# A two-block transformer on one Trainium2 core: the second block's first mixer as one stage, and the overflow quads of the experts before the last regular quad

## The chip, the core and the metric

The kernel runs on one core of a Trainium2 chip. The core has TensorE (matrix products into PSUM), VectorE and ScalarE (elementwise work on PSUM and SBUF), GpSimd, and SyncE, whose queue here issues the weight loads. The engines run their own instruction streams and meet only at semaphores. The metric is the device time of one launch in microseconds (us). All data are float32.

## What is computed

A first pair of layers (attention, then pooling, each followed by a mixture of 32 experts with top-2 routing) is followed by a second pair (mixer A+B with a dense feed-forward, then mixer C with another). 256 tokens, 1024 channels. The parts that matter here, cut:

```python
def expert_block(args):                      # per layer, tokens sorted by expert
    xb, e = args
    return (jax.nn.silu(xb @ w1[e]) * (xb @ w3[e])) @ w2[e]

def s5_ssm(u, ...):                          # 32 groups of 16 channels, 64 complex states each
    bu_re = jnp.einsum('blgp,gnp->blgn', ug, bb_re)
    bu_im = jnp.einsum('blgp,gnp->blgn', ug, bb_im)
    _, _, x_re, x_im = lax.associative_scan(_complex_affine_combine, (a_seq_re, a_seq_im, bu_re, bu_im), axis=1)
    y = jnp.einsum('blgn,gpn->blgp', x_re, c_re) - jnp.einsum('blgn,gpn->blgp', x_im, c_im)
    return y + d_skip * ug

def mixer_ab(x, ...):
    proj = x @ w_in                          # three blocks of 512: xm, zm, us
    xc = jax.nn.silu(causal_dwconv(xm, conv_w, conv_b))
    q, k, v = block-diagonal maps (4x4 blocks) of xc, xc, xm
    gates = jnp.concatenate([q, k, v], axis=-1) @ w_if + b_if
    h = mlstm_chunkwise(q, k, v, gates[..., :4], gates[..., 4:])       # 4 heads of 128
    hn = layer norm of h over each head, * mh_gain
    out_m = (hn + skip * xc) * jax.nn.silu(zm)
    y = jax.nn.gelu(s5_ssm(us, ...))
    out_s = y * jax.nn.sigmoid(y @ w_glu + b_glu)
    return jnp.concatenate([out_m, out_s], axis=-1) @ w_out
```

## The kernel before

The program is a list of stages. In each a function per engine gives its instructions; at its end every engine drains and adds one to `stage_done`, and all wait for all four before the next stage (`run_stages`, L236). Weights stream from HBM through a ring of six slots of 2 MB (`ring_buffer`); SyncE issues every load when `weights_used`, which TensorE increments, shows that the slot's last unit was consumed.

**Experts** (`experts(layer, lead)`, twice). Each expert has a block of 32 token slots; four blocks make a quad, so one quad fills the 128 partitions. A quad needs 12 units of 2 MB (24 MB), twice the ring. Eight regular quads (`FIRST_QUADS`) hold all 32 experts; quad 1 is the wide quad, whose four experts each get a second block (`_b`) on the same weights. For experts with still more tokens there are four overflow quads (`MORE // QUAD`). Whether one is live is only known at run time (`quad_live`, written by `table_dve`). Every engine runs `each_quad`: a loop over quads 2 to 7, then a loop over the four overflow quads that reads `quad_live`; for a dead one it only drains and increments each semaphore of the quad once. SyncE does the same in `load_experts`, where a dead quad waits until TensorE has consumed all 96 units. TensorE's quad is: turn the weights of the picks (L1283), `up` of w1 (two phases) and w3 (two phases, L1272), gather the next quad's tokens (L1245), turn the product (L1288), `down` (two phases, L1297), `combine` (L1311) into PSUM banks 0 to 3. In the wide quad `up` and `down` run for both blocks before a unit's slot is released.

**Mixer A+B** (`mixer_ab`) is seven stages: projections (L1877; VectorE copies the tiles, then convolves, L1901 and L1904), q/k/v and gates (L1932 to L1941; VectorE takes the 12 tiles, L1949), gate sums and the running maximum (L1970 to L2008), four heads (L2030 to L2080), layer norm (L2098 to L2124), the state space in four quarters (L2147 to L2200), and the GLU (L2214 to L2226). In a quarter TensorE makes real and imaginary inputs of four groups of pairs (`states`), VectorE turns them by the angle of each time step (L2173 to L2179), runs eight scans (L2182, L2183), turns back (L2185 to L2188) and adds (L2189, L2190), and TensorE multiplies by C (`outputs`, L2156, L2157); VectorE adds the skip (L2194) and ScalarE applies GELU (L2200). `project_out` (L1754) follows.

`chain["dve"]` (`v(...)` below) makes an instruction increment a semaphore and the engine wait for it before the next.

## Time and profile before

| | us |
|---|---|
| median of 3 runs | 2293.22 (2293.07 to 2293.73) |
| the profiled execution's own time | 2287.05 |
| span of the profiled execution | 2285.2 |
| busy share of the span: TensorE, VectorE, ScalarE, GpSimd | 76%, 23%, 9%, 4% |
| of it, the seven stages of mixer A+B (1348.34 to 1549.80) | 201.5 |

The profile is of one execution. Times in it count from the start of the span. TensorE's `PEclk` is the granted clock: 1.00 is 2.4 GHz, 0.50 is 1.2 GHz.

### The profile page before, as it was taken

The page shows a single profiled execution, that of the slowest core. Times are in us where ns is not written, and L with a number is a line of the kernel's source. Part 1 is how long each engine was busy: PE and PEld are TensorE (multiplying, and loading weights), DVE is VectorE, ACT ScalarE, POOL GpSimd, SP SyncE. Part 2 cuts the span into 40 slices and gives each one's busy share as a digit, 9 for nine tenths or more (in the row PEclk, how much of TensorE's full clock was granted, in tenths as well). Part 3 has the DMA queues.
Part 4 walks back from the last instruction along what each step waited for, and adds up shares of the span by engine and source line. Part 5 has one row for each costly group of instructions (what it writes and reads, how often), then busy time and mean ns, then how long its engine had stood idle before and what let it go on. Part 6 is the DMA issues. An engine that isn't in the chain of part 4 may idle for free. (4 is left out here: it accounts for less than half of the span.)

```text
span 2285.2 us, 22430 instructions
## 1 busy us (share of the span) xinstructions
PE 1728.7 (76%) x8954; PEld 997.7 (44%) x8955; DVE 522.8 (23%) x1188; ACT 208.2 (9%) x489; POOL 93.5 (4%) x120
## 2 busy tenths in 40 slices
PE   6999867766666566876666658218999989889998
PEld 3655533321222343322222247114886476648863
DVE  1214352110111164111011132882000023320001
ACT  1011110000000110000000011002000122110000
POOL 1010010000000037000000000000000000000000
PEclk9999989887878778887787878558999999789999
DMA  9969179999999748999999951006335334124330
GB/s 367 378 247 388 74 297 389 397 422 422 422 422 422 295 174 336 381 420 422 422 422 422 386 172 42 1 10 220 119 117 188 142 137 146 63 83 147 111 129 19
DMA packets 125764, 581.02 MB, mean 254 GB/s; under 512 B 14004, under 2 KB 18392, under 8 KB 70264
## 3 DMA queue, kind: packets, MB, share of 16 engines
q1 hardware_dynamic: 120416, 573.90, 62.8%
q10 hardware_dynamic: 4344, 3.25, 0.5%
q0 software_dynamic: 928, 2.79, 0.4%
q8 instruction: 56, 0.92, 0.2%
q14 instruction: 20, 0.16, 0.0%
HBM read 578.86 MB, written 1.05 MB: 254 GB/s over the span
## 5 line engine op out<-in xcount | busy, mean ns | idle before, releaser
L1272 PE MATMUL ps<-ring_buffer,arena 128*32 128x512 f32 x2048 | 312.5, 767 | 198.9 <-DMA ring_buffer<-in_exp_w 196.1
L1796 PE MATMUL ps<-hT,ring_buffer 128*128 128x256 f32 x1408 | 310.9, 383 | 4.1 <-issue 2.6
L1796 PEld LDWEIGHTS ps<-hT,ring_buffer 128*128 128x128 f32 x1408 | 269.4, 192 | 45.5 <-issue 6.3
L1272 PEld LDWEIGHTS ps<-ring_buffer,arena 128*32 128x32 f32 x2048 | 85.0, 136 | 412.6 <-issue 336.2
L1297 PE MATMUL ps<-ring_buffer,arena 128*32 128x512 f32 x1088 | 155.9, 726 | 101.2 <-DMA ring_buffer<-in_exp_w 90.1
L1804 PE MATMUL ps<-ring_buffer,arena 128*128 128x512 f32 x352 | 154.2, 595 | 3.0 <-DVE arena L1837 1.9
L1297 PEld LDWEIGHTS ps<-ring_buffer,arena 128*32 128x32 f32 x1088 | 41.0, 130 | 204.9 <-issue 196.7
L1466 DVE TENSOR_TENSOR arena<-arena,ps 128x512 f32<-128x512 f32 x18 | 19.2, 1069 | 439.9 <-PE ps L1272 439.9
L1804 PEld LDWEIGHTS ps<-ring_buffer,arena 128*128 128x128 f32 x352 | 65.9, 190 | 90.4 <-issue 87.8
L1245 PE MATMUL ps<-arena,xn 128*128 128x128 f32 x640 | 81.9, 289 | 12.4 <-DVE arena L1436 12.4
L1245 PEld LDWEIGHTS ps<-arena,xn 128*128 128x128 f32 x640 | 78.5, 203 | 27.9 <-issue 22.2
L2276 PE MATMUL ps<-hT,ring_buffer 128*128 128x256 f32 x384 | 85.9, 385 | 1.9 <-issue 1.0
L1837 DVE TENSOR_TENSOR arena<-arena,ps 128x256 f32<-128x256 f32 x44 | 18.5, 421 | 296.9 <-ACT arena L1831 296.9
L2276 PEld LDWEIGHTS ps<-hT,ring_buffer 128*128 128x128 f32 x384 | 73.6, 193 | 14.7 <-issue 3.5
L1387 ACT ACTIVATE arena<-ps,mod,gain 128x128 f32<-128x128 f32 x72 | 27.1, 457 | 436.5 <-PE ps L1245 436.5
L713 PE MATMUL ps<-hT,ring_buffer 128*128 128x256 f32 x256 | 58.6, 391 | 3.1 <-ACTq L236 2.5
L1754 PE MATMUL ps<-ring_buffer,hT 128*128 128x512 f32 x128 | 58.1, 613 | 2.1 <-DVEq L236 1.9
L1311 PE MATMUL ps<-arena 128*128 128x512 f32 x128 | 59.3, 605 | 0.0
L1482 DVE TENSOR_TENSOR arena<-ps,gates 128x512 f32<-128x512 f32 x16 | 11.1, 692 | 198.9 <-PE ps L1297 198.9
L498 PE MATMUL ps<-ring_buffer,arena 128*32 128x512 f32 x384 | 49.6, 637 | 8.0 <-DMA ring_buffer<-in_ada_w 7.1
L713 PEld LDWEIGHTS ps<-hT,ring_buffer 128*128 128x128 f32 x256 | 50.0, 197 | 13.0 <-issue 3.3
L2156 PE MATMUL ps<-ring_buffer,arena 128*32 128x256 f32 x32 | 4.4, 634 | 57.3 <-DVE ring_buffer L2190 57.3
(493 smaller groups left out, 1566.9 us busy)
## 6 DMA issues: line engine op xcount, KB each, us to landing
ring_buffer<-in_exp_w SPq DMA_DIRECT2D x384, 1024.0 KB, 18.5
ring_buffer<-in_ffn_w SPq DMA_DIRECT2D x30, 2048.0 KB, 9.0
ring_buffer<-in_ada_w SPq DMA_DIRECT2D x24, 2048.0 KB, 12.8
ring_buffer<-in_c_w_in SPq DMA_DIRECT2D x8, 2048.0 KB, 9.1
ring_buffer<-in_attn_w_in SPq DMA_DIRECT2D x6, 2048.0 KB, 16.8
ring_buffer<-in_ab_w_in SPq DMA_DIRECT2D x3, 2048.0 KB, 12.8
ring_buffer<-in_ffn_w SPq DMA_DIRECT2D x6, 1024.0 KB, 9.2
ring_buffer<-in_attn_w_o SPq DMA_DIRECT2D x2, 2048.0 KB, 12.9
```

The lines of the kernel that those rows point to most:

```text
L498: pe.matmul(ps[g * WIDE:(g + 1) * WIDE, COND, :], spread_c[:, 2 * pair + k, row:row + WIDE], w[:, k, 512 * n:512 * (n + 1)], start=(first ...
L713: ins = pe.matmul(ps[:, n % BANKS, 0:S], w[:, k, j * P:(j + 1) * P], hT[:, k, :], start=(k == 0), stop=(k == KD - 1))
L1245: ins = pe.matmul(ps[:, BXA + k // 4, (k % 4) * P:(k % 4 + 1) * P], xn[:, t, k * P:(k + 1) * P], pick[:, t, :], start=(t == 0), stop=(t == ...
L1272: ins = pe.matmul(ps[c, bank, :], tokens[:, 4 * phase + k, c], halves[j][:, k, :], start=(phase == 0 and k == 0), stop=(phase == 1 and k = ...
L1297: ins = pe.matmul(ps[c, bank, :], tokens[:, 2 * phase + k, c], halves[j][:, k, half * 512:(half + 1) * 512], start=(phase == 0 and k == 0) ...
L1311: ins = pe.matmul(ps[:, 2 * half + t, :], weights[:, t, :], values[:, half * 512:(half + 1) * 512], start=opens, stop=False, skip_group_ch ...
L1387: return eng.activation(o, src, ACT.Identity, scale=G[:, k:k + 1], bias=H[:, k:k + 1])
L1466: dve.tensor_tensor(prod.rearrange("c (h k p) -> c h p k", h=2, k=2), gated.rearrange("c (h p k) -> c h p k", h=2, k=2), ps[:, bank, :].re ...
L1754: ins = pe.matmul(ps[:, 2 * c + t, :], fT[:, k, t * P:(t + 1) * P], w[:, k, :], start=(k == 0), stop=(k == KD - 1))
L1796: ins = pe.matmul(ps[:, f % 8, i * S:(i + 1) * S], w[:, k, j * P:(j + 1) * P], hT[:, k, :], start=(k == 0), stop=(k == KD - 1))
L1804: ins = pe.matmul(ps[:, 2 * half + t, :], aT[:, r + k, t * P:(t + 1) * P], w[:, k, 512 * half:512 * half + 512], start=(r + k == 0), stop= ...
L2276: ins = pe.matmul(ps[:, n % 8, 0:S], w[:, k, j * P:(j + 1) * P], hT[:, k, :], start=(k == 0), stop=(k == KD - 1))
```

## The change

1. **Mixer A+B is one stage.** The projection order is us, xm, zm. ScalarE now copies every projection, q/k/v and gate tile out of PSUM (`take_tile`), through three rotating banks (4 to 6). VectorE runs the four state-space quarters with the steps of the other branch in between; TensorE's instructions are interleaved by hand. GELU is one instruction over all four quarters, and the GLU's sigmoid follows the layer norm's square root.
2. **Last sums by TensorE.** VectorE no longer makes the two sums at the end of a quarter (L2189, L2190 before). It writes four products, and TensorE accumulates four products with C in place of two.
3. **Dead quads moved.** The overflow quads come before quad 7, on every engine and on SyncE, with semaphores of their own for their weights (`more_landed`, `more_used`); quad 7 stands alone behind the loop. Several pairs of semaphores became one that counts twice.
4. **Wide quad reordered.** Both blocks of a phase run one after the other (w3 phase 0 of a, then of b, then phase 1 of each; `down` likewise), and block b has a product buffer of its own.
5. **Small loads moved.** The q/k/v block weights, `w_if` and `b_if` are loaded by GpSimd during the second experts, where ScalarE loaded them at the mixer's start.

```diff
             def each_quad(eng, quad, signals, steps=0):
-                with eng.Fori(WIDE_QUAD + 1, FIRST_QUADS) as i:
+                with eng.Fori(WIDE_QUAD + 1, FIRST_QUADS - 1) as i:
                     quad(i, i + 1)
                 eng.wait_ge(table_ready, 2 * layer + 2)
                 with eng.Fori(0, QUADS - FIRST_QUADS) as more:
...
                     with eng.Else():
-                        for s in signals:
-                            eng.drain().then_inc(s, 1)
+                        for s, count in signals:
+                            eng.drain().then_inc(s, count)
...
+                quad(FIRST_QUADS - 1, BLOCKS - 1)
...
                     with sp.Else():
-                        sp.wait_ge(weights_used, n0 + UNITS * FIRST_QUADS + UNITS * i)
+                        sp.wait_ge(more_used, m0 + RING + UNITS * i)
                         for slot in range(RING):
-                            sp.drain().then_inc(weights_landed[slot], 64)
-                        sp.drain().then_inc(weights_used, UNITS)
+                            sp.drain().then_inc(more_landed[slot], 64)
+                        sp.drain().then_inc(more_used, UNITS)
+                sp.wait_ge(more_used, m0 + RING + UNITS * MORE_QUADS)
+                load_quad(FIRST_QUADS - 1)
```

```diff
+                def outputs(c):
+                    pe.wait_ge(x_ready, c + 1)
+                    if c:
+                        pe.wait_ge(y_taken, c)
+                    for i, (n, part) in enumerate(((0, z[:, 0]), (1, z[:, 1]), (1, t_re), (0, t_im))):
+                        for q in range(4):
+                            ins = pe.matmul(ps[32 * q:32 * q + 32, Y, 0:S], CT[:, n, c, 32 * q:32 * q + 32], part[:, q, :],
+                                            start=(i == 0), stop=(i == 3))
+                    ins.then_inc(y_ready, 1)
...
+                def turn_out(c):
+                    co, si = rotation(c)
+                    dve.tensor_tensor(z[:, 0], t_re, co, ALU.mult)
+                    v(dve.tensor_tensor(z[:, 1], t_im, co, ALU.mult))
+                    dve.tensor_tensor(t_re, t_re, si, ALU.mult)
+                    dve.scalar_tensor_tensor(out=t_im, in0=t_im, scalar=-1.0, in1=si, op0=ALU.mult, op1=ALU.mult).then_inc(x_ready, 1)
...
+                turned_in(0)
+                scans(0, range(4))
+                turn_out(0)
+                for n in range(4):
+                    convolve(n)
+                take_y(0)
...
+                turn_out(1)
+                forget()
+                take_y(1)
+                log_forget()
...
+                scans(2, range(4))
+                sums()
+                turn_out(2)
+                running_max()
+                take_y(2)
...
+                weigh(0)
+                scans(3, range(2))
+                weigh(1)
+                finish(0)
+                scans(3, range(2, 4))
+                weigh(2)
+                finish(1)
+                turn_out(3)
+                weigh(3)
+                finish(2)
+                skip()
+                finish(3)
+                take_y(3)
+                statistics()
+                normed()
+                for n in range(3):
+                    glu_out(n)
+                mlstm_out()
+                glu_out(3)
```

On TensorE, the end of the first experts. Before, the overflow loop (L1229) comes behind the last `combine` (L1311), and the pooling of the next stage (L1585) waits behind it:

```order
L1311 MATMUL ps<-arena 128x512
L1232 UNCONDITIONAL_BRANCH
L1234 UNCONDITIONAL_BRANCH
L1229 REGISTER_ALU
L1229 COMPARE_AND_BRANCH
L1585 MATMUL ps<-consts,xn 128x128 [waits norm_scaled,stage_done]
```

Now quad 7 (its first `up` is L1306, its `combine` L1345) stands between that loop and the next stage:

```order
L1260 REGISTER_ALU
L1260 COMPARE_AND_BRANCH
L1317 MATMUL ps<-consts,arena 128x128 [waits quad_xa_taken,quad_weighted]
L1317 MATMUL ps<-consts,arena 128x128
L1306 MATMUL ps<-ring_buffer,arena 32x512 [waits weights_landed3,weights_landed4,quad_y_taken,quad_xb_taken]
...
L1345 MATMUL ps<-arena 128x512 [waits quad_y_taken]
L1345 MATMUL ps<-arena 128x512
L1620 MATMUL ps<-consts,xn 128x128 [waits norm_scaled,stage_done]
```

The overflow loop moved from behind the last quad to in front of it.

On VectorE, from the end of one quarter to the next quarter's first product. Before:

```order
L2185 TENSOR_TENSOR ring_buffer<-xn,arena 128x1024 [waits dve_step]
L2186 TENSOR_TENSOR ring_buffer<-ring_buffer,arena 128x1024
L2187 TENSOR_TENSOR xn<-xn,arena 128x1024 [waits dve_step]
L2188 TENSOR_TENSOR ring_buffer<-ring_buffer,arena 128x1024 [waits dve_step]
L2189 TENSOR_TENSOR ring_buffer<-ring_buffer 128x1024 [waits dve_step]
L2190 TENSOR_TENSOR ring_buffer<-ring_buffer,xn 128x1024 [waits dve_step]
L2194 SCALAR_TENSOR_TENSOR gates<-arena,cols,ps 128x256 [waits s5_y_ready]
L2173 TENSOR_TENSOR ring_buffer<-ps,arena 128x1024 [waits s5_bu_ready,s5_y_ready]
```

Now, behind the second quarter:

```order
L2146 TENSOR_TENSOR ring_buffer<-xn,arena 128x1024 [waits dve_step]
L2147 TENSOR_TENSOR ring_buffer<-gates,arena 128x1024
L2148 TENSOR_TENSOR xn<-xn,arena 128x1024 [waits dve_step]
L2149 SCALAR_TENSOR_TENSOR gates<-gates,arena 128x1024
L2172 TENSOR_TENSOR small<-small,consts 128x16 [waits ab_tile_taken]
L2173 TENSOR_SCALAR arena<-small 128x8 [waits dve_step]
L2174 TENSOR_TENSOR arena<-small,arena 128x8 [waits dve_step]
L2175 TENSOR_SCALAR arena<-small 128x8
L2153 SCALAR_TENSOR_TENSOR xn<-arena,cols,ps 128x256 [waits s5_y_ready,dve_step]
L2179 TENSOR_TENSOR arena<-arena 128x8 [waits log_sigmoid_ln]
L2127 TENSOR_TENSOR ring_buffer<-ps,arena 128x1024 [waits s5_y_ready,s5_bu_ready]
```

Two 128x1024 sums and two waits on VectorE's own semaphore are gone, and the forget gate's small steps stand between the products and the wait for `y_ready`.

On TensorE, from the gates (L2025) to the sums of the forget gate (L2038), all one stage now:

```order
L2025 MATMUL ps<-consts,ring_buffer 128x8 x23
L1960 MATMUL ps<-ring_buffer,arena 32x256 [waits s5_y_taken,s5_x_ready]
L1960 MATMUL ps<-ring_buffer,arena 32x256 x7
L1960 MATMUL ps<-xn,arena 32x256 x4
L1960 MATMUL ps<-gates,arena 32x256 x4
L1941 MATMUL ps<-hT,ring_buffer 128x256 [waits ab_tile_taken,weights_landed0]
L1941 MATMUL ps<-hT,ring_buffer 128x256 x7
...
L2038 MATMUL ps<-arena,consts 128x4 [waits ab_lf_ready,ab_tile_taken]
```

The third projection block (zm) and the last `states` stand between the second quarter's `outputs` and the gate sums.

## Rows read from the trace of the kernel before

**Rows 1.** Windows of the mixer: start:end, length, busy of five engines, PEclk, DMA share, GB/s.

```profile
1348.34:1449.45 101.11, 75.25 (x370) 65.05 (x370) 39.67 (x121) 12.76 (x22) 0.00 (x0) 0.82 0.15 48
1449.45:1539.35 89.90, 16.28 (x128) 7.81 (x128) 77.67 (x84) 2.95 (x5) 0.00 (x0) 0.50 0.00 0
1539.35:1549.80 10.45, 9.39 (x32) 7.59 (x32) 1.70 (x4) 3.18 (x5) 0.00 (x0) 0.78 0.59 202
```

**Rows 2.** Timeline, VectorE, a quarter: start, us, what [idle before, releaser].

```profile
1495.26 1.22 DVE L2173 TENSOR_TENSOR ring_buffer<-ps,arena 128x1024 f32<-128x1024 f32 x1
...
1502.30 0.69 DVE L2182 TENSOR_TENSOR_SCAN xn<-arena,ring_buffer 128x256 f32<-128x256 f32 x1
...
1507.10 1.23 DVE L2185 TENSOR_TENSOR ring_buffer<-xn,arena 128x1024 f32<-128x1024 f32 x1
...
1509.50 1.23 DVE L2187 TENSOR_TENSOR xn<-xn,arena 128x1024 f32<-128x1024 f32 x1
...
1516.61 0.48 DVE L2194 SCALAR_TENSOR_TENSOR gates<-arena,cols,ps 128x256 f32<-128x256 f32 x1 [2.11 <-PE ps L2157]
```

**Rows 3.** Timeline, TensorE, the last sums of that quarter (`outputs`).

```profile
1514.56 1.10 PE L2156 MATMUL ps<-ring_buffer,arena 128*32 128x256 f32 x8 [12.52 <-DVE ring_buffer L2190]
```

**Rows 4.** Groups by line, mixer before 1449.4: busy us, mean ns, idle before.

```profile
L1877 PE MATMUL ps<-hT,ring_buffer 128*128 128x256 f32 x192 | 44.4, 394 | 1.3 <-ACTq L236 1.0 <-issue 0.3
...
L1949 DVE TENSOR_SCALAR ring_buffer<-ps 128x256 f32<-128x256 f32 x12 | 5.1, 425 | 3.7 <-PE ps L1932 3.7
...
L1908 DVE COPY arena<-ps 128x256 f32<-128x256 f32 x4 | 1.7, 425 | 18.8 <-PE ps L1877 18.8
...
L1898 DVE COPY arena<-ps 128x256 f32<-128x256 f32 x4 | 1.7, 424 | 14.9 <-PE ps L1877 14.9
...
L1953 DVE COPY arena<-ps 128x512 f32<-128x512 f32 x2 | 1.3, 687 | 1.4 <-PE ps L1935 1.4
```

**Rows 5.** Timeline, ends of both experts: TensorE's last work, SyncE's and VectorE's next.

```profile
770.10 3.71 PE L1311 MATMUL ps<-arena 128*128 128x512 f32 x8
...
777.53 8.81 SPq L1188 DMA_DIRECT2D ring_buffer<-in_exp_w  x12
784.50 1.88 DVE L1564 TENSOR_TENSOR x<-x,ps 128x512 f32<-128x512 f32 x3 [13.54 <-PEq L236]
...
1331.21 2.48 DVE L1564 TENSOR_TENSOR x<-x,ps 128x512 f32<-128x512 f32 x4 [13.46 <-PEq L236]
```

**Rows 6.** Timeline, TensorE, end of quad 6 and start of quad 7, second experts.

```profile
1261.90 3.71 PE L1272 MATMUL ps<-ring_buffer,arena 128*32 128x512 f32 x32
1271.70 6.58 PE L1272 MATMUL ps<-ring_buffer,arena 128*32 128x512 f32 x32 [6.08 <-DMA ring_buffer<-in_exp_w]
```

**Rows 7.** Windows: wide quads of both experts, quads in between, mixer's small loads.

```profile
390.00:400.00 10.00, 6.97 (x64) 2.11 (x56) 1.91 (x3) 0.00 (x0) 0.00 (x0) 1.00 0.96 396
410.00:420.00 10.00, 10.00 (x70) 4.16 (x63) 1.39 (x2) 0.00 (x0) 0.00 (x0) 1.00 0.72 281
935.00:940.00 5.00, 5.00 (x48) 1.59 (x50) 1.59 (x2) 0.00 (x0) 0.00 (x0) 1.00 0.84 310
955.00:960.00 5.00, 5.00 (x52) 1.59 (x48) 0.54 (x2) 0.00 (x0) 0.00 (x0) 1.00 0.47 152
1020.00:1260.00 240.00, 154.56 (x956) 56.33 (x955) 29.98 (x65) 8.40 (x20) 0.00 (x0) 0.81 1.01 422
1352.00:1354.00 2.00, 2.00 (x9) 1.70 (x8) 0.00 (x0) 1.16 (x1) 0.00 (x0) 0.81 0.63 31
```

**Rows 8.** Timeline, ScalarE, loads of activation tables at the gate.

```profile
1411.93 1.28 ACT L1970 ACT_TABLE_LOAD   x1 [15.47 <-DVE arena L1981]
1413.22 0.21 ACT L1970 ACTIVATE arena<-arena 128x8 f32<-128x8 f32 x1
```

**Rows 9.** Windows behind the mixer: first feed-forward's matrix products, and the rest.

```profile
1590.00:1800.00 210.00, 207.52 (x823) 157.40 (x824) 9.27 (x22) 9.71 (x23) 0.00 (x0) 0.99 0.38 138
1800.00:2285.00 485.00, 443.87 (x1675) 307.76 (x1673) 84.45 (x196) 64.87 (x163) 0.00 (x0) 0.94 0.30 106
```

More of the change, by code:

```diff
@@ L1419, in quads_act @@
                 wide_quad(WIDE_QUAD)
[L1420 removed]
+                each_quad(act, quad, ((silu_done, 1), (xb_taken, 1)))
             def quads_dve(dve):
@@ new lines, in all_pe @@
+                ins.then_inc(tile_ready, 1)
+                outputs(1)
+                w = ring.take(pe, ("ab_in", 1))
+                for j in range(4):
+                    project(w, j, Z + j)
+                    if j == 1:
+                        states(3)
+                release(pe)
+                pe.wait_ge(tile_taken, Z + 4)
+                pe.wait_ge(lf_ready, 1)
+                pe.matmul(ps[:, 4, 0:4], const("upto"), t1[:, 0, :], start=True, stop=True)
+                pe.matmul(ps[:, 4, 4:8], ones, t1[:, 0, :], start=True, stop=False)
```

788 lines of the change are left out of this document (407 added, 381 removed).

## The prediction

> **What bounds the kernel now.** I read the windows first: which engine is busy in each stretch, and at which clock. Then the timeline of the one that sets its end. The kernel has three kinds of stretch here.
>
> Between the wide quad and quad 7 of the experts the loads are the bound: DMA share 1.01 at 422 GB/s, while TensorE has 154.56 busy of 240 us [rows 7]. A quad's 24 MB take 59.6 us at that rate, and TensorE is idle 20 us in each. A microsecond in which the loads stop is a microsecond lost. One of TensorE or VectorE costs nothing as long as the ring stays full.
>
> Mixer A+B takes 101.11 + 89.90 + 10.45 = 201.46 us [rows 1], and no engine is busy throughout. In the first window TensorE is busy 75 us and VectorE 40, in the second TensorE 16 and VectorE 78. One works while the other waits, and in the second window TensorE stands at PEclk 0.50, the lower level. The stages' barriers force that order, the data do not: the two branches share only the input and the output. The reader is to see that VectorE's work of both windows, run without a break, is about 120 us.
>
> Behind it TensorE is the bound, 207.52 of 210 us at PEclk 0.99, later 443.87 of 485 at 0.94 [rows 9].
>
> **The merged mixer.** I take VectorE as its chain and add up what it has to do.
>
> A quarter: from the first product at 1495.26 to L2194 at 1516.61 are 21.35 us [rows 2]. Of these 2.11 are the wait for TensorE. The first two products of the turn back take 1509.50 - 1507.10 = 2.40, so all four end at 1511.9; L2189 and L2190 fill the rest up to TensorE's start at 1514.56 [rows 3], some 2.6, and they go. L2194 itself, overlapped, is 0.4. A quarter is 21.35 - 2.11 - 2.6 + 0.4 = 17.1, four are 68.4. (Inside, the inputs and scans keep their time: 7.04 to the first scan, 4.80 for eight scans.)
>
> The other branch: VectorE has 39.67 + 1.70 busy in the first and third window [rows 1]. L1949, L1908, L1898 and L1953 go to ScalarE: 5.1 + 1.7 + 1.7 + 1.3 = 9.8 [rows 4]. 31.6 remain. Together 100.0 us of VectorE work.
>
> Waits that remain, about 21 us:
> - The start. VectorE needs two of the four tiles of `us` (the first quarter's input), and one group of `states`. L1877 has 44.4 us in 12 tiles, 3.7 each [rows 4]: two tiles are 7.4, one more hop through ScalarE. 8.
> - `y`. From TensorE's start of `outputs` to L2194 are 2.05 now, at the low clock, for eight products of 32 columns on four column groups side by side [rows 3]. Twice as many are 3.8 at the low clock, 1.9 at the high one. The order puts convolution behind the first quarter (covers it), the forget gate behind the second, the running maximum behind the third, which covers part of each; the last is followed by the skip. 5 in all.
> - The gate sums. They stand on TensorE behind the zm block (four tiles, some 14 us) and the third `states`. VectorE has the second quarter's take, input and scans to do meanwhile, which is less. Between 3 and 8, taken at 4 to 5.
> - The tail (square root, sigmoid, the last tile) and the steps between engines: 2 and 2.
>
> That is 121 us for 201.5: **-80.5**. TensorE's own work there, each window times its clock, is 75.25 x 0.82 + 16.28 x 0.50 + 9.39 x 0.78 = 77 us at the high level, 81 with the doubled `outputs`. It fits into 121 only if it runs mostly at the high level. I take that it does, since the first window, with a TensorE that is busy 74%, had 0.82 already. With no half clock at all the pieces VectorE waits for would give 115, with half clock in them 128. ScalarE adds 9.8 to some 19 us of work: no bound. The feed-forward's loads now start at the end of the mixer and not 10 us before; the stage behind, `project_out`, covers them. Nothing.
>
> ScalarE loads one table more. The trace shows a load of 1.28 us with the next activation at once behind it [rows 8], and in my sum it hides beside VectorE. The Trainium skill, "ScalarE: Activation LUTs", section "What ACT_TABLE_LOAD costs", gives a drain of 1380 ns on top, 2.66 us per switch; by it the switch to the sigmoid in the tail would make the sum 1.4 us longer. No such gap stands in this row.
>
> **Dead quads.** From the last `combine` (770.10 + 3.71 = 773.81) to VectorE's next stage (784.50) pass 10.7 us in the first experts [rows 5]. In the second VectorE starts at 1331.21, with the same wait (13.46 against 13.54), so I take the same gap. In it the engines walk through four dead quads and a barrier. For the barrier alone I leave 0.5, between 0 and 1. So -10.2 each, **-20.4**, if the walk is hidden where it stands now. There TensorE starts quad 7's `up` at 1261.90, then has 6.08 us idle until units 2 and 3 land and starts them at 1271.70 [rows 6]. Ten us later `up` would start at 1272, when four units have landed; two pieces of 3.71 of unhindered work put it behind by about 7, and with 20 us idle per quad it has caught up at unit 4 or 5. The loads are not held up, as SyncE's walk (7.4 us from 770.10 to 777.53) passes while five units, some 25 us, are in flight, and the slots of units 0 and 1 come free at 1276 to 1280, before the queue runs dry at about 1282. This margin is thin, 2 to 6 us. The loads for the next stage, which start earlier now, were complete in time before: nothing more.
>
> **Wide quad.** With 422 GB/s as the rate of a full queue, the first experts lose 10 x (1 - 396/422) = 0.6 and 10 x (1 - 281/422) = 3.3, the second 5 x (1 - 310/422) = 1.3 and 5 x (1 - 152/422) = 3.2 [rows 7]. In these TensorE is busy through (10.00 of 10.00, 5.00 of 5.00): the ring is full, since both phases of block a run before block b touches the unit. In the new order a slot is free one piece earlier. 3.9 + 4.5, and neighbouring losses of under 1: between 0 and 9.5, taken at the upper end, **-8.5**, since TensorE is the only thing that the queue waits for there.
>
> **Small loads.** At the mixer's start they ran at share 0.63 [rows 7] beside the projections, waited for by no one. Now they lie in the stream of the second experts, where the share is 1.01. 31 GB/s at 0.63 says that their packets are small and cost more time than bytes. For a few us of that, 0 to 3; taken **+1.0**.
>
> **Sum.** -80.5 - 20.4 - 8.5 + 1.0 = -108.4. The profiled execution's 2287.05 becomes 2178.7; the median of before, 2293.22, stands 6.2 above it, so the time is **2185 us**, 4.7% less.
>
> **The rivals.**
>
> *The clock stays low in the mixer.* TensorE would work in pieces with breaks, as in the second window, which is at 0.50 throughout. If only the pieces that VectorE waits for run at it, the start costs 7 more, `y` 3 and the gate sums 4: mixer 135, time **2199**. If all does, 81 x 2 = 162 and some 19 of waits: mixer 181, **2245**. Against: about 81 of 121 us are work for TensorE and the projections are queued to fill its gaps.
>
> *The dead quads are not hidden.* If quad 7's slots come free after the queue has run dry, or SyncE's drains last as long as the transfers in flight, the stream stops for about what the gap at the end cost. Up to 20 us come back: **2205**. For it speaks the thin margin. Against: 20 us of idle TensorE per quad, and TensorE waits for the loads at that place, not the reverse.
>
> *The edit does not do what it says.* VectorE's order is a list by hand. If one place waits for a step that is late (gate sums, heads), the merged stage keeps the sum of both waits; the first window has some 60 us in which VectorE is idle, and if a quarter of them came back, the time would be **2200**.
>
> *Slower.* TensorE is busy 207.52 + 443.87 = 651.4 us behind the mixer, at a mean of 0.955. A mixer that keeps TensorE busy for 121 us on end, after experts in which the clock was 0.81 [rows 7], removes the rest that the second window gave. If this lowered the clock behind, 108.4 us would be lost when 651.4 x (0.955/c - 1) reaches them, c = 0.82; below that the kernel is slower than before, at 0.80 (+126) **2311**. Against: the clock is 0.99 in 207 us of uninterrupted work, so work does not lower it here.
>
> **How the numbers follow.** My forecast, all parts about as priced, has 0.71, and by itself 2175 to 2194. The clock rival has 0.09 (nearly all at 2199), the dead quads 0.10, the order of VectorE 0.09, slower 0.01. The range shall hold 0.8. Below, mixer 115, wide quads 9.5 and small loads at nothing give 2177; I go to 2172, since waits of the mixer (21 us of guesses between rows) may be 5 fewer. Above it takes in the three middle rivals, up to 2210. Faster by over 0.2%, 4.6 us, about what a measurement of this kernel can tell from no change, 0.98; within it 0.01; slower by more 0.01.
>
> **What would show it.** Right: from the mixer's first `us` tile to `project_out` about 121 us, with VectorE busy 100 of them and PEclk above 0.9 in TensorE's busy stretches; VectorE's waits for `outputs` at most 2 each, that for the gate sums 3 to 8; under 1 us between the last `combine` and VectorE's first step of the next stage; quad 7's first `up` ten us late, but its later ones on time; DMA share near 1 through both wide quads and through the end of quad 6. Wrong: a break in the loads behind quad 6, a mixer over 130, VectorE idle in it in one long piece, or a lower clock behind 1590.

## The result, and the profile after

| | before | after |
|---|---|---|
| median | 2293.14 us (2292.31 to 2293.73, 4 runs) | 2182.19 us (2176.27 to 2188.47, 4 runs) |
| span of the profiled execution | 2285.2 | 2186.4 |
| first `up` of the first experts | 301.14 | 307.96 |
| from there to the last `combine` | 468.96 | 465.70 |
| to VectorE's next stage | 14.40 | 3.78 |
| to the first `up` of the second experts | 52.97 | 59.91 |
| to the `combine` of quad 6 | 420.58 | 417.47 |
| to that of quad 7 | 58.86 | 61.59 |
| to VectorE's next stage | 14.30 | 3.79 |
| to the mixer's first product | 17.13 | 16.88 |
| the mixer, to `project_out` | 201.48 | 117.47 |
| from there to the end of the span | 735.38 | 731.85 |

The ratio is 0.9517 (95% interval 0.9485 to 0.9548): 111 us less. The forecast was 2185. The rows of the table are starts of instructions in the timelines, and each stretch begins where the one above ends. The last row takes the span to 0.1 us. The way to the first `up` differs as much between two profiles of the changed kernel (see "The changed kernel again"). Two other stretches got longer: the one between the experts, and quad 7 of the second.

The merged mixer, in the windows of the changed kernel (columns as in [rows 1]), with the two windows in the wide quads and the one behind quad 6 that the forecast named:

```profile
1337.08:1454.55 117.47, 96.34 (x595) 77.21 (x595) 96.66 (x179) 28.51 (x53) 0.00 (x0) 0.90 0.11 41
410.00:420.00 10.00, 10.00 (x67) 3.63 (x60) 2.77 (x4) 0.00 (x0) 0.00 (x0) 0.96 1.02 420
950.00:960.00 10.00, 10.00 (x68) 3.98 (x61) 2.77 (x4) 0.00 (x0) 0.00 (x0) 1.00 1.01 419
1275.00:1280.00 5.00, 5.00 (x52) 1.37 (x48) 0.18 (x1) 0.00 (x0) 0.00 (x0) 1.00 0.82 310
```

TensorE and VectorE are both busy 96 of 117 us, where they took turns in [rows 1]; PEclk is 0.90 where it was 0.50 in the long middle window. In the wide quads the loads run at 420 GB/s while TensorE is busy through ([rows 7]: 281 and 152). Behind quad 6 they drop to 310 for 5 us, which was not forecast.

VectorE's waits in the mixer, from its timeline (the six that are over 0.7 us):

```profile
1345.44 2.36 DVE L2127 TENSOR_TENSOR ring_buffer<-ps,arena 128x1024 f32<-128x1024 f32 x2 [6.06 <-PE ps L1951]
...
1390.97 0.48 DVE L2153 SCALAR_TENSOR_TENSOR xn<-arena,cols,ps 128x256 f32<-128x256 f32 x1 [2.84 <-PE ps L1960]
...
1407.54 0.17 DVE L2183 COPY arena<-ps 128x8 f32<-128x8 f32 x1 [4.29 <-PE ps L2040]
...
1416.34 0.48 DVE L2153 SCALAR_TENSOR_TENSOR xn<-arena,cols,ps 128x256 f32<-128x256 f32 x1 [2.42 <-PE ps L1960]
...
1442.57 0.48 DVE L2153 SCALAR_TENSOR_TENSOR xn<-arena,cols,ps 128x256 f32<-128x256 f32 x1 [0.77 <-PE ps L1960]
...
1450.25 0.43 DVE L2252 TENSOR_TENSOR hT<-xn,hT 128x256 f32<-128x256 f32 x1 [1.30 <-ACT hT L2110]
```

L2127 is the first product of a quarter, L2153 takes `y`, L2183 the gate sums. The first quarter's `y` is not there: the convolution covers it.

The end of quad 6 and quad 7 of the second experts on TensorE:

```profile
1254.82 3.70 PE L1345 MATMUL ps<-arena 128*128 128x512 f32 x8
1271.27 0.66 PE L1317 MATMUL ps<-consts,arena 128*128 128x128 f32 x2 [12.75 <-issue]
1271.86 11.69 PE L1306 MATMUL ps<-ring_buffer,arena 128*32 128x512 f32 x96
1289.27 6.35 PE L1306 MATMUL ps<-ring_buffer,arena 128*32 128x512 f32 x32 [5.72 <-DMA ring_buffer<-in_exp_w]
```

The walk through the dead quads takes 12.75 us. TensorE then does three pieces in a row (x96) and waits for a load ahead of the fourth, at 1289.27. It has caught up with the loads. But the loads slowed down behind quad 6, between 21 and 24 us behind the start of its `combine`, and the last pair of the quad lands late: its products start 61.7 us behind those of quad 6 (1310.52 - 1248.77), where it was 59.7 before (1311.55 - 1251.88). Of these 2.1 us the 5 us window explains 5 x (1 - 310/422) = 1.3; the rest was not taken apart.

Between the experts, on TensorE. Before:

```profile
811.83 1.97 PE L622 MATMUL ps<-consts,xn 128*128 128x128 f32 x16 [3.73 <-DVE xn L606]
815.00 5.31 PE L1026 MATMUL ps<-arena,hT 128*128 128x32 f32 x32 [1.20 <-ACT hT L591]
```

After, with VectorE's first step of that stage:

```profile
777.44 2.48 DVE L1599 TENSOR_TENSOR x<-x,ps 128x512 f32<-128x512 f32 x4 [2.94 <-PEq L237]
```

```profile
784.42 0.77 PE L1620 MATMUL ps<-consts,xn 128*128 128x128 f32 x2 [7.06 <-DVE xn L607]
...
808.20 3.67 PE L623 MATMUL ps<-consts,xn 128*128 128x128 f32 x16 [3.74 <-DVE xn L607]
813.03 7.01 PE L1033 MATMUL ps<-arena,hT 128*128 128x32 f32 x32 [1.16 <-ACT hT L592]
```

VectorE starts 7.06 us earlier than in [rows 5], and TensorE's pooling too. Then the same 16 transposes take 3.67 us for 1.97 and the same router products 7.01 for 5.31. At 820 us both kernels are level again. The windows show why; before, 10 to 20 us behind the stage's start:

```profile
794.50:799.50 5.00, 5.00 (x38) 4.97 (x37) 1.47 (x4) 0.99 (x3) 0.00 (x0) 0.81 1.01 418
799.50:804.50 5.00, 5.00 (x25) 4.41 (x24) 1.29 (x2) 0.97 (x3) 0.00 (x0) 1.00 1.02 423
```

After, in the same place of the program:

```profile
787.44:792.44 5.00, 5.00 (x25) 5.00 (x25) 0.76 (x3) 0.84 (x2) 0.00 (x0) 0.50 1.02 418
792.44:797.44 5.00, 5.00 (x21) 4.57 (x21) 0.72 (x2) 0.84 (x2) 0.00 (x0) 0.60 0.59 244
```

The granted clock is at its lower level for most of these 10 us (0.50, 0.60), where it had been mostly at the higher (0.81, 1.00). Over the whole stretch between the experts TensorE is idle 21.0 us before and 20.7 after, but busy 32.0 and 39.2 with the same 188 matmuls in the trace: the longer time is in the products, not in waits.

### The profile page after: what moved, and what is told of

The parts are those of the page before. It is cut to its first block and busy times, and to the rows that moved or that the text cites. A ratio compares the mean times of both kernels' runs of the same rounds, so it can differ in the third digit from the quotient of the medians.

```text
span 2186.4 us, 22473 instructions
## 1 busy us (share of the span) xinstructions
PE 1731.5 (79%) x9018; PEld 1000.1 (46%) x9019; DVE 501.8 (23%) x1168; ACT 218.1 (10%) x510; POOL 97.9 (4%) x125
## 5 line engine op out<-in xcount | busy, mean ns | idle before, releaser
L1306 PE MATMUL ps<-ring_buffer,arena 128*32 128x512 f32 x2048 | 309.6, 763 | 170.6 <-DMA ring_buffer<-in_exp_w 167.9
L1306 PEld LDWEIGHTS ps<-ring_buffer,arena 128*32 128x32 f32 x2048 | 82.1, 135 | 384.8 <-issue 325.0
L1789 PE MATMUL ps<-ring_buffer,hT 128*128 128x512 f32 x128 | 59.7, 627 | 3.3 <-DVEq L237 3.0
L1345 PE MATMUL ps<-arena 128*128 128x512 f32 x128 | 59.3, 605 | 0.0
L1436 ACT ACTIVATE arena<-ps 128x512 f32<-128x512 f32 x18 | 10.8, 597 | 416.7 <-PE ps L1306 416.7
```

Of the source, the lines that this page charges most:

```text
L1306: ins = pe.matmul(ps[c, bank, :], tokens[:, 4 * phase + k, c], halves[j][:, k, :], start=(phase == 0 and k == 0), stop=(phase == 1 and k = ...
L1345: ins = pe.matmul(ps[:, 2 * half + t, :], weights[:, t, :], values[:, half * 512:(half + 1) * 512], start=opens, stop=False, skip_group_ch ...
L1789: ins = pe.matmul(ps[:, 2 * c + t, :], fT[:, k, t * P:(t + 1) * P], w[:, k, :], start=(k == 0), stop=(k == KD - 1))
```

## The experiments

Times on other chips lie a few us apart, and the runs of one kernel too, so the stretches of the profiles are compared as well as the medians. This table has them for all kernels (us; the columns are the stretches of the table above, "in" being the first `up` of the first experts).

| kernel | in | first experts | gap | between | second, to quad 6 | quad 7 | mixer | behind |
|---|---|---|---|---|---|---|---|---|
| before | 301.14 | 468.96 | 14.40 | 52.97 | 420.58 | 58.86 | 201.48 | 735.38 |
| changed | 307.96 | 465.70 | 3.78 | 59.91 | 417.47 | 61.59 | 117.47 | 731.85 |
| changed, again | 301.23 | 465.73 | 3.79 | 59.88 | 417.67 | 61.34 | 117.47 | 731.81 |
| quads back | 301.48 | 463.05 | 13.56 | 52.93 | 417.39 | 58.84 | 117.49 | 731.85 |
| wide back | 306.78 | 470.13 | 3.79 | 59.07 | 421.81 | 61.46 | 119.70 | 731.85 |
| sums back | 300.17 | 465.82 | 3.79 | 59.92 | 417.58 | 61.42 | 126.67 | 742.83 |
| gates early | 301.62 | 465.75 | 3.79 | 59.87 | 417.53 | 61.45 | 115.20 | 730.78 |
| loads late | 305.70 | 465.60 | 3.79 | 56.37 | 413.97 | 61.62 | 117.58 | 731.85 |
| filler | 303.96 | 465.54 | 3.79 | 53.46 | 417.46 | 61.24 | 117.48 | 731.88 |
| rest | 302.79 | 463.36 | 13.86 | 56.09 | 417.56 | 61.22 | 117.45 | 731.82 |
| two overflow quads | 299.10 | 462.59 | 3.79 | 59.93 | 414.71 | 60.65 | 117.57 | 731.86 |
| three edits | 302.14 | 463.46 | 3.79 | 52.30 | 414.78 | 61.62 | 117.39 | 740.50 |
| four edits | 303.72 | 465.52 | 3.79 | 53.55 | 414.89 | 63.15 | 112.53 | 730.34 |

**The dead quads back behind quad 7.**

```diff
-                last = float(P * FIRST_QUADS)
+                last = float(P * (FIRST_QUADS + 1))
-                v(dve.tensor_tensor(at_start, at_start, tmp_e, ALU.add))
...
-                with sp.Fori(1, FIRST_QUADS - 1) as i:
+                with sp.Fori(1, FIRST_QUADS) as i:
                     load_quad(i)
...
+                sp.wait_ge(weights_used, n0 + UNITS * FIRST_QUADS)
                 with sp.Fori(0, MORE_QUADS) as i:
...
-                load_quad(FIRST_QUADS - 1)
...
-                with eng.Fori(WIDE_QUAD + 1, FIRST_QUADS - 1) as i:
+                with eng.Fori(WIDE_QUAD + 1, FIRST_QUADS) as i:
...
-                quad(FIRST_QUADS - 1, BLOCKS - 1)
```

> The changed kernel with the overflow quads behind quad 7 again, on every engine and in the queue of the loads. Theory A (the dead quads' walk is hidden but for about 2 us of lost loads each time): from the last combine of the experts to VectorE's next stage 10.7 us again (0.1 in the changed kernel), twice; the loads run through the end of quad 6 without a break (now 310 GB/s in 5 us), which gives back 2.1 each; 17 us more in sum, if nothing else moves. Theory B (a rest of TensorE raises its granted clock behind it): the stretch from the end of the first experts to the second router's scores, 43.0 us in the changed kernel against 36.2 before, is some 6.8 us shorter again, so only about 10 us more in sum. Between 2190 and 2202.

2191.53 us median (2188.51 to 2196.67), ratio 0.9553 (0.953 to 0.9577). The gaps come back, 13.56 and 13.21 us to VectorE's next stage against 3.79; quad 7 takes 58.84 for 61.59; the first experts are 2.65 shorter; and between the experts the stretch is 52.93, as before. TensorE there:

```profile
764.53 3.70 PE L1343 MATMUL ps<-arena 128*128 128x512 f32 x8
...
785.06 0.77 PE L1618 MATMUL ps<-consts,xn 128*128 128x128 f32 x2 [16.83 <-DVE xn L607]
...
808.55 5.33 PE L1033 MATMUL ps<-arena,hT 128*128 128x32 f32 x32 [1.20 <-ACT hT L592]
...
831.02 10.51 PE L1304 MATMUL ps<-ring_buffer,arena 128*32 128x512 f32 x96 [1.35 <-ACT arena L1417]
```

It rests 16.83 us and the router products take 5.33 again. In the end the move is worth, from "in" to the end of the mixer, 1153.37 - 1146.56 (the changed kernel again) = 6.8 us, and the marks say where: -9.8 and -9.4 for the gaps, +2.65 and +2.6 up to the `combine` of quad 7, where the loads break, +7.0 between the experts. At the first experts -9.8 stands against +2.65 and +7.0, so nothing is left of the gain. The break itself is in the windows of every kernel with four overflow quads ahead of quad 7, and in neither experts' stage of this one. Theory B, that a rest of TensorE lets the clock rise, fits this run; it is taken further below.

**The wide quad in its old order.**

```diff
                     up(i, 4, 0, xgT, BU, u_ready, None, one=weights_used)
-                    up(i, 4, 0, xgT_b, BXB, u_ready)
                     up(i, 4, 1, xgT, BU, u_ready, None)
+                    up(i, 4, 0, xgT_b, BXB, u_ready)
+                    pe.wait_ge(prod_done, i0 + b + 1)
+                    turn_prod(BG, prod)
                     up(i, 4, 1, xgT_b, BXB, u_ready)
...
                     down(i, 0, prodT, (BU, BG), None, one=weights_used)
+                    down(i, 1, prodT, (BU, BG), None)
                     down(i, 0, prodT_b, (BXB, BXA))
-                    down(i, 1, prodT, (BU, BG), None)
                     down(i, 1, prodT_b, (BXB, BXA))
```

> The changed kernel with the wide quad's pieces in the old order (w3 both phases of a before b, down likewise). Theory: the loads stop again while the ring is full, 281 GB/s in a 10 us window of the first wide quad where the changed kernel has 420, and 5.4 us come back in the first experts, 2.7 in the second: 8 more. Rival: the new order gained nothing by itself, the shift between the traces came from the clock in the stages before; then within 1 us of the changed kernel.

2192.68 us median (2189.11 to 2197.42), ratio 0.9551 (0.9528 to 0.9573). The first experts take 4.4 more, the second 4.3: 8.7. The windows of its two wide quads:

```profile
410.00:420.00 10.00, 10.00 (x84) 3.03 (x80) 1.85 (x3) 0.00 (x0) 0.00 (x0) 0.85 0.68 266
955.00:965.00 10.00, 10.00 (x87) 3.10 (x79) 2.77 (x4) 0.00 (x0) 0.00 (x0) 0.96 0.68 265
```

The loads stand still again beside a TensorE that is busy through. Its mixer is 2.2 longer, with a first block of 32 products that took 9.30 us for 7.17.

**The sums at a quarter's end on VectorE.**

```diff
-                    dve.tensor_tensor(t_re, t_re, si, ALU.mult)
-                    dve.scalar_tensor_tensor(out=t_im, in0=t_im, scalar=-1.0, in1=si, op0=ALU.mult, op1=ALU.mult).then_inc(x_ready, 1)
+                    v(dve.tensor_tensor(t_re, t_re, si, ALU.mult))
+                    v(dve.tensor_tensor(t_im, t_im, si, ALU.mult))
+                    v(dve.tensor_tensor(z[:, 0], z[:, 0], t_im, ALU.subtract))
+                    dve.tensor_tensor(z[:, 1], z[:, 1], t_re, ALU.add).then_inc(x_ready, 1)
```

with `outputs` multiplying the two parts of `z` alone.

> The changed kernel with the two sums at a quarter's end on VectorE again and eight products per quarter on TensorE. Theory (VectorE is the chain of the mixer): 4 x 2.6 = 10.4 more on VectorE, less 1.0 to 1.6 for each of the three visible waits for outputs, so the mixer takes 117.4 + 6 to 7 us. Rival (TensorE sets the end of the stage): mixer unchanged within 1 us.

2196.17 us median (2190.48 to 2200.68), ratio 0.9563 (0.9539 to 0.9586). The mixer takes 126.67, 9.2 more: more than the 6 to 7 expected, since only 0.8 of waiting went while VectorE has 10.0 more to do. The three waits for `y` fell by 3.8 us together (1.55, 0.71 and none, for 2.84, 2.42 and 0.77), but that for the gate sums rose to 5.83 from 4.29, and the 24 products of the GLU took 7.09 us for 5.42. The windows of the mixer, and of 20 us in mixer C:

```profile
1329.40:1456.07 126.67, 96.78 (x530) 78.58 (x531) 106.67 (x187) 28.54 (x53) 0.00 (x0) 0.84 0.11 38
1876.07:1896.07 20.00, 20.00 (x84) 14.25 (x82) 7.23 (x24) 3.60 (x20) 0.00 (x0) 0.50 0.00 1
```

VectorE is the chain, as forecast. And behind the mixer, in instructions that are the same in both kernels, this execution is 11.0 us longer: in mixer C TensorE is busy 20 of 20 us at 0.50, where the changed kernel has 0.99 at the same distance from the mixer's end. The kernel before stood at 0.81 there. Behind the mixer TensorE is idle 52.8 us in this kernel and 53.3 in the changed one, and busy 690.0 for 678.5.

**The gate sums earlier.**

```diff
                 for j in range(4):
+                    if j == 2:
+                        pe.wait_ge(tile_taken, Z + 2)
+                        pe.wait_ge(lf_ready, 1)
+                        pe.matmul(ps[:, 4, 0:4], const("upto"), t1[:, 0, :], start=True, stop=True)
+                        pe.matmul(ps[:, 4, 4:8], ones, t1[:, 0, :], start=True, stop=False)
+                        pe.matmul(ps[:, 4, 4:8], const("upto"), t1[:, 1, :], start=False, stop=True).then_inc(b_ready, 1)
                     project(w, j, Z + j)
...
-                pe.wait_ge(lf_ready, 1)
-                pe.matmul(ps[:, 4, 0:4], const("upto"), t1[:, 0, :], start=True, stop=True)
```

> The changed kernel with the sums of the forget gate two tiles earlier on TensorE, in the middle of the zm block. Theory: VectorE's wait of 4.29 us for them goes to 0 and the mixer takes 113 us instead of 117.4. Rival: the wait turns up behind it (the transposes of a behind the last zm tiles, the third outputs), and the mixer loses less than 1 us.

2188.19 us median (2172.04 to 2193.51), ratio 0.9525 (0.9495 to 0.9556): by its median no different. The mixer takes 115.20, 2.3 less and not 4.3. VectorE's waits:

```profile
1384.62 0.48 DVE L2155 SCALAR_TENSOR_TENSOR xn<-arena,cols,ps 128x256 f32<-128x256 f32 x1 [2.91 <-PE ps L1960]
...
1404.03 0.48 DVE L2155 SCALAR_TENSOR_TENSOR xn<-arena,cols,ps 128x256 f32<-128x256 f32 x1 [0.71 <-PE ps L1960]
...
1431.05 0.48 DVE L2155 SCALAR_TENSOR_TENSOR xn<-arena,cols,ps 128x256 f32<-128x256 f32 x1 [1.56 <-PE ps L1960]
...
1439.90 0.42 DVE L2254 TENSOR_TENSOR hT<-xn,hT 128x256 f32<-128x256 f32 x1 [2.41 <-ACT hT L2112]
```

The wait of 4.29 us is gone and that for the third `y` is 0.71 for 2.42, so up to there VectorE gained 6.0 (1416.34 - 1337.08 against 1404.03 - 1330.72). Behind it 3.7 were lost again. TensorE at the mixer's end, in this kernel:

```profile
1432.77 8.32 PE L1991 MATMUL ps<-xn,ring_buffer 128*128 128x256 f32 x24 [1.78 <-ACT xn L2107]
```

and in the changed one:

```profile
1444.29 5.42 PE L1991 MATMUL ps<-xn,ring_buffer 128*128 128x256 f32 x24 [1.79 <-ACT xn L2105]
```

The same 24 products of the GLU took 8.32 us for 5.42.

**The small loads at the mixer's start.** The five `pool.dma_start` of the second experts go, and stand ahead of the first `take_tile` as `act.dma_start`.

> The changed kernel with the small loads of q/k/v, w_if and b_if issued by ScalarE at the mixer's start again. Theory (they cost the saturated stream of the second experts 2.4 us, which is what the traces leave for them: first up to the last pair of quad 6 is 411.4 us in the changed kernel, 414.4 before and 416.8 with the wide quad's order undone): the same stretch takes 409.0, and the mixer stays at 117.4 since VectorE waits 6 us there for the first states anyway. Rival: VectorE waits for the loads ahead of its first product and the mixer grows by as much or more.

2181.72 us median (2179.06 to 2184.45), ratio 0.9507 (0.9474 to 0.954). To quad 6 the second experts take 413.97 us, 3.5 less, and in the kernels with three and four edits below 414.8 and 414.9, 2.6 to 2.9 less. To the last pair of quad 6, the stretch of the expectation, it is 407.6 us for 411.4, where 409.0 was expected. VectorE's first steps in the mixer:

```profile
1334.43 1.90 DVE L2260 TENSOR_TENSOR ring_buffer<-consts 128x512 f32<-128x512 f32 x3 [6.18 <-DMA consts<-in_ab_b_if]
1336.25 2.35 DVE L2127 TENSOR_TENSOR ring_buffer<-ps,arena 128x1024 f32<-128x1024 f32 x2
```

VectorE waits 6.18 us for the loads, and its first product comes 8.4 us behind the mixer's start (1327.87), as in the changed kernel (1345.44 - 1337.08). There is no margin, but the mixer stays at 117.58. Between the experts this kernel has 56.37, in instructions that are the same as in the changed one.

**Products in TensorE's pause between the experts.**

```diff
             def pe_(pe):
+                for i in range(32):
+                    pe.matmul(ps[:, 7, 0:P], ident, const("upto"), start=True, stop=True)
                 pe.wait_ge(norm_signals[3], TT * u)
```

> The changed kernel with 32 products of 128 columns that nobody reads, on TensorE, at the start of the stage between the two experts, where it idles 7 us. Theory (the granted clock falls in that pause and stays low through the pooling): TensorE starts the pooling at the high clock, and from the stage's start to the second experts' first up pass 52 us or less instead of 59.9. Rival (TensorE is slowed for work done before, as in the experts' end): work in the pause makes it worse, over 60 us.

2172.32 us median (2169.16 to 2177.35), ratio 0.9458 (0.9425 to 0.9491). Between the experts 53.46 us pass, 6.4 fewer, where 52 or less was expected. The two windows that answer to those above, 10 to 20 us behind the stage's start:

```profile
783.29:788.29 5.00, 5.00 (x36) 4.72 (x36) 0.88 (x2) 1.68 (x4) 0.00 (x0) 1.00 1.01 419
788.29:793.29 5.00, 5.00 (x27) 4.45 (x26) 1.55 (x3) 1.15 (x2) 0.00 (x0) 1.00 0.63 259
```

The clock is at its higher level. TensorE is idle 13.8 us in the stretch for 20.7, and busy 39.7, of which the added products (32 in the code, x64 in the trace; where this text quotes a row, its number of products is the trace's) are 7.4: the others take 32.3 us for 39.2. The pooling starts 7.27 us behind VectorE's first step for 6.97, so the added products delay it by 0.3. The router products behind it still take 7.01 us:

```profile
798.47 3.06 PE L623 MATMUL ps<-consts,xn 128*128 128x128 f32 x16 [3.70 <-DVE xn L607]
802.69 7.01 PE L1033 MATMUL ps<-arena,hT 128*128 128x32 f32 x32 [1.16 <-ACT hT L592]
...
826.75 10.51 PE L1306 MATMUL ps<-ring_buffer,arena 128*32 128x512 f32 x96 [0.96 <-ACT arena L1419]
```

**A longer rest in its place.**

```diff
             def dve_(dve):
+                for i in range(8):
+                    chain["dve"](dve.tensor_tensor(hT[:, 0:4, :], hT[:, 4:8, :], hT[:, 4:8, :], ALU.add))
                 add_from_psum(dve)
```

> The changed kernel with eight 128x1024 additions that nobody reads, on VectorE, ahead of its first step between the two experts, so that TensorE rests some 10 us longer there, as it did before. Theory (a longer rest lets the clock rise within the pooling, as in the kernel before and with the quads back): the stretch to the second experts' first up is 59.9 + 10 - 7 = 63 us. Rival (it is the place in the program or the change elsewhere, not the rest): 70 us.

One run, 2186.75 us. The gap is 13.86 and the stretch behind it 56.09, so together 66.2 us for the 63 and the 70 of the two theories: the additions cost 10.1 and 3.8 came back. TensorE rests 17.14 us there, nearly as in the kernel before (17.66); but 10 to 20 us behind VectorE's start its clock is 0.50 and 0.67, and of the two groups shown above only the router products are nearly as short as before:

```profile
786.99 0.77 PE L1620 MATMUL ps<-consts,xn 128*128 128x128 f32 x2 [17.14 <-DVE xn L607]
...
813.62 5.45 PE L1033 MATMUL ps<-arena,hT 128*128 128x32 f32 x32 [1.20 <-ACT hT L592]
```

So the length of the rest alone does not decide. Seven kernels have the same instructions between the experts and the same gap of 3.8; five took 59.9 us, one 59.07 and one 56.37. What is shown: in the ten kernels without products in this pause TensorE is idle 20.7 to 21.0 us of the stretch, and what differs is its busy time for the same 188 matmuls, 32.0 us at a mean clock of 0.73 up to 39.2 at 0.66. Filling the pause took the stretch to 52.3 to 53.6 us three times out of three. What sets the clock in the unfilled cases stays open.

**Half the overflow quads.** `MORE = S // SLOTS` for `2 * S // SLOTS`.

> The changed kernel with room for two overflow quads where it has four (this leaves out the third and fourth; none of the four is live with these inputs). Theory: TensorE's pause at quad 7 goes from 12.7 us to some 7.5, the first up of quad 7 starts before the queue of loads runs dry, and the time from the last pair of quad 6 to that of quad 7 goes from 61.7 to 59.6 us in the second experts. Rival: the 2 us are lost to TensorE's own catching up or to the queue of the loads walking through the dead quads, then 60.7 or more.

One run, 2173.07 us.

```profile
1240.12 3.70 PE L1345 MATMUL ps<-arena 128*128 128x512 f32 x8
1251.81 0.66 PE L1317 MATMUL ps<-consts,arena 128*128 128x128 f32 x2 [7.99 <-issue]
1252.40 8.59 PE L1306 MATMUL ps<-ring_buffer,arena 128*32 128x512 f32 x64
```

TensorE's pause is 7.99 us for 12.75, 2.4 a dead quad, so four dead quads are some 9.5 of the 12.75 and 3.2 are not theirs. From the last pair of quad 6 (1234.73) to that of quad 7 (1294.59) pass 59.9 us for 61.75: nearly the 59.6 of the theory, and no window behind quad 6 shows a break, in either experts' stage. So the break of the loads was due to the length of the walk. Both experts are also 3 us shorter elsewhere (462.59; 414.71), which the edit was not meant for. In the first experts "rest" and "three edits", with all four overflow quads, have 463.4 and 463.5, so it need not come from the edit; in the second 2.4 of it lie in the wide quad (72.06 us for 74.48 from the `combine` ahead of it to its own). This was not taken apart.

**Three edits together** (gates early, loads late, filler) **and four** (the same, and 16 products in TensorE's pause ahead of the fourth head):

```diff
                 for h in range(4):
...
+                    if h == 3:
+                        for i in range(16):
+                            pe.matmul(ps[:, LG[0], 0:P], ident, const("upto"), start=True, stop=True)
                     mix(h)
```

> The changed kernel with three of the edits together: gate sums two tiles earlier, small loads at the mixer's start, 32 products in TensorE's pause between the experts. Theory (they act in different stages, so they add): 2.3 + 3.5 + 6.4 = 12 us under the changed kernel, 2170, with the stretch between the experts at 53.5, the second experts up to quad 6 at 414.0 and the mixer at 115.2. Rival (the clock gives back elsewhere what it gains here): a gain of 6 us or less, with the difference in TensorE's granted clock behind the mixer or between the experts.

> As the one before, and 16 products of 128 columns that nobody reads in TensorE's pause of 5.5 us ahead of the fourth head's sums, close to the mixer's end. Theory (the outputs and the GLU behind that pause run at the low clock, 8.32 us for the 24 products of the GLU that take 5.42 at the high one): the mixer takes 112 us instead of 115.2. Rival (the pause is not what lowers the clock): 115, or more if they delay the fourth head.

Three: 2178.83 us median (2175.68 to 2183.09), ratio 0.9487 (0.9464 to 0.9509). Four: 2170.19 (2164.73 to 2174.33), ratio 0.9445 (0.9421 to 0.9469). In the first, two stretches gain what their edits did alone (52.30 between, 414.78 in the second experts). The mixer does not: it takes 117.39 us where "gates early" took 115.20. Its first 32 products take 9.29 us for 7.17, at a clock of 0.57 in the first 5 us where the changed kernel has 1.00, and VectorE's first product comes 10.5 us behind the start for 8.4. "Wide back" lost its 2.2 us in the same place. And 8.7 us are lost behind the mixer. Its window in mixer C:

```profile
1856.40:1876.40 20.00, 20.00 (x83) 14.00 (x83) 6.50 (x22) 3.01 (x17) 0.00 (x0) 0.50 0.00 1
```

That is the rival of the expectation: the same instructions met a lower clock, and by the medians 2.7 of the 12 us are left (2178.83 for 2181.57). By the profile this kernel is 12.3 us ahead of the changed one at the mixer's end (1134.26 from "in" for 1146.56), 2.3 of them in the first experts, where no edit was made. In the second the first 32 products are back at 7.17 us, the mixer takes 112.53 (112 expected), 2.7 less than in "gates early", and behind it pass 730.34. TensorE at its end:

```profile
1420.76 0.49 PE L1983 MATMUL ps<-arena,hT 128*128 128x129 f32 x2 [1.93 <-DVE hT L2209]
...
1426.11 7.11 PE L1989 MATMUL ps<-xn,ring_buffer 128*128 128x256 f32 x24 [2.56 <-ACT xn L2112]
```

The fourth head starts 1.93 us behind the added products, so they delay nothing. The outputs run at the high clock (1.07 us for the first group, 1.94 without them); the GLU still takes 7.11 us for 5.42.

**The changed kernel again.**

> The changed kernel once more, unchanged, beside the two others, for its spread. The start of the first experts was seen between 299 and 308 us of the span in kernels that have the same instructions up to there. Theory: this is what spreads the runs of one kernel; the runs lie between 2172 and 2190, and the other marks of its profile (59.9 between the experts, 417.5 for the second experts up to quad 6, 117.5 for the mixer, 731.85 behind it) come out as in the first profile. Rival: the spread comes from several of these stretches.

2181.57 us median (2176.68 to 2184.52), ratio 0.9497 (0.9473 to 0.9521). All stretches come out within 0.3 us of the first profile; only "in" differs, 301.23 for 307.96. The windows between 255 and 260 us of the span, again and then in the first profile:

```profile
255.00:260.00 5.00, 5.00 (x14) 2.51 (x14) 0.63 (x4) 0.00 (x0) 0.00 (x0) 1.00 0.82 341
```

```profile
255.00:260.00 5.00, 5.00 (x11) 2.66 (x12) 0.62 (x4) 0.00 (x0) 0.00 (x0) 0.71 0.92 383
```

At 240 us of the span the two executions are 0.7 us apart, at 271 us 2.4, at the first experts' router products (283 us) 4.0, and at the first `up` 6.7. Up to there TensorE is idle 40.5 and 40.4 us and busy 267.4 and 260.9, with 1364 matmuls in both. The spread of the runs of one kernel is, as far as two profiles can tell, the granted clock between the attention's last products and the experts' first `up`, ahead of the stages that this change was meant for.

The four edits together have the lowest median: 2170.19 beside 2181.57 for the changed kernel in the same batch, and the intervals of the two ratios do not meet. From "filler" alone (2172.32, 0.9425 to 0.9491) they can't be told apart.

## Why the prediction was right, and where it was not

**The mixer, -80.5 forecast, -84.0 measured.** The sum of VectorE's work (100.0) came out as 96.66, and the waits (21) as 117.47 - 96.66 = 20.8. One by one: the start 8.4 for 8, of which VectorE waits only 6.1, since 2.3 are steps of its own; `y` 2.84 + 2.42 + 0.77 = 6.0 for 5; the gate sums 4.29 for 4 to 5; 4.4 remain for the tail and the steps between engines, for 4. The doubled `outputs` had been priced at 3.8 us at the low clock and 1.9 at the high one, from their start to L2153; they took 3.7 in the changed kernel (1416.34 - 1412.62) and 2.0 in "gates early" (1404.03 - 1402.03). "Sums back" shows that VectorE is the chain: 10.0 more on it made the mixer 9.2 longer. The forecast put the price of the two sums at 2.6 a quarter, 10.4 in all.

**The clock in the mixer.** 0.90 over the stage, so the rival of a low clock did not happen as a whole; but it is there in pieces. The second and third `outputs` and the first group of the fourth ran at the low level (1.93, 1.93 and 1.94 us for a group of x16 that takes 1.07 in the first quarter), and "gates early" lost 3.7 of 6.0 us to it.

**The tail.** The loads of activation tables at the mixer's end, on ScalarE:

```profile
1445.76 1.28 ACT L2110 ACT_TABLE_LOAD   x1
1447.05 0.47 ACT L2110 ACTIVATE hT<-ps,cols 128x256 f32<-128x256 f32 x1
```

The sigmoid starts 0.01 us behind the load of 1.28, and the load 0.02 us behind the activation before it (1445.53, 0.21 us), so the sum by the row stood. The drain of 1380 ns that the Trainium skill ("ScalarE: Activation LUTs", "What ACT_TABLE_LOAD costs") adds to a switch is not in this row either.

**Dead quads, -20.4 forecast, -6.8 measured.** This is the step that failed. The gaps went as forecast (9.8 and 9.4 of the 10.2 each, against "quads back", where the merged semaphores had already shortened the walk by 0.8 and 1.1). Two things were missed. First, the margin called thin did not hold: TensorE's pause is 12.75 us, not 10, the loads ran at 310 GB/s for 5 us, and some 2.6 us were lost in each experts' stage. Counted from the start of quad 6's `combine` (1258.05 before, 1254.82 now), the forecast had quad 7's `up` at 14 us and the queue dry at 24; `up` came at 17 and the loads fell off at 21. The forecast had the mechanism among its rivals, but priced it as all or nothing. Second, 7.0 us went between the experts, where TensorE had worked at the high clock after its long rest and now did not. "Quads back" shows that the move costs them; that the length of the rest is the reason is not shown, since "rest" gave back 3.8. Outside the mixer the forecast looked for a lower clock behind it only, some 670 us further on. It took [rows 5] for the place where the gain is made, and did not ask what the same idle time did for the stage behind it.

**Wide quad, -8.5 forecast, -8.7 measured** by "wide back", from the loads' standing time alone.

**Small loads, +1.0 forecast, +2.6 to 3.5 measured.** The range was 0 to 3. The row gave a share of 0.63 with 31 GB/s [rows 7], which says that the loads cost time and not bytes; the price should have been taken at the upper end, since in that stretch nothing hides them.

**What is left.** -84.0 - 6.8 - 8.7 + 3 is -96.5. Between the marks, the kernel before against the changed one "again" has 1984.1 - 1878.4 = 105.7. Of the 9.2 between them 3.5 are behind the mixer, in mixer C, by the clock (735.38 for 731.85), 1.9 the shorter walk of the merged semaphores in "quads back", and the rest, some 3.8, lies in the experts and was not taken apart. Errors did cancel here: 13.6 too much for the dead quads and 2 too little for the small loads stand against 3.5 in the mixer, 3.5 behind it and 5.7 in edits priced at nothing. The total was right by that as much as by its largest term.

**The rival of the other side.** It asked for a clock under 0.82 behind the mixer; its mean there is 0.96, as against 0.95 before. A lower clock behind the mixer does occur on a small scale: 8.7 and 11.0 us in two kernels that differ from others only ahead of it. The reason that the forecast gave for it, a TensorE without rest in the mixer, does not fit: in "sums back", which lost the 11.0, TensorE is idle 29.9 us in the mixer, and 21.1 in the changed kernel.

## What to carry to other kernels

When stages of two engines that take turns are merged, add up the busy time of the engine with the longer chain from the rows before, and a guess for each wait: here that gave 121 us for a measured 117.5. Which step of the other engine comes too late can be read from the waits that are left. An idle gap that is removed is not worth its length where TensorE's clock behind it depends on how it came there: compare the same instructions behind the gap in both traces, and try products that nobody reads in the pause. A walk of many empty steps that is moved beside a stream of loads can outlast the loads in flight, as here with four dead quads and not with two, so shorten the walk first.

## What the runs showed of the hardware that was not expected

The same instructions between the two experts took from 52.3 to 59.9 us (13 profiles), and those behind the mixer from 730.3 to 742.8, and TensorE's idle time in them was the same within 0.3 us (in the ten kernels without products in the pause) and 0.7 us: what differed was its busy time, with the granted clock. Some values came back within 0.1 us in several kernels, 59.9 in five and 731.8 in eight; others came once. 32 products without use, 7.4 us of work in a pause of 7.1, made the changed kernel faster by 6.4 us in its stretch. A rest of 17.14 us in place of 7.06 gave back 3.8 us of the 7 in one kernel, and the rest of 16.83 in another all of it.
